# Paged attention: each group's latent page request in two halves, the second behind a key turn

## What is computed

```python
ckv_past = cache_ckv[l, page_table].reshape(db, past_len, KV_LORA)      # 8 x 8192 x 256
kr_past = cache_krope[l, page_table].reshape(db, past_len, MLA_ROPE)    # 8 x 8192 x 32

def mla_sample_attention(q_nope, q_rope, c_kv, k_rope, ckv_past, krope_past, w_uk, w_uv):
    q_lat = jnp.einsum('bthn,lhn->bthl', q_nope, w_uk)
    s_past = (jnp.einsum('bthl,bpl->bhtp', q_lat, ckv_past)
              + jnp.einsum('bthr,bpr->bhtp', q_rope, krope_past))
    ...
    s = jnp.concatenate([s_past, s_new], axis=-1) * scale
    p = jax.nn.softmax(s, axis=-1)
    lat = (jnp.einsum('bhtp,bpl->bthl', p[..., :P], ckv_past)
           + jnp.einsum('bhts,bsl->bthl', p[..., P:], c_kv))
    return jnp.einsum('bthl,lhv->bthv', lat, w_uv)
```

## Time and profile before

| | |
|---|---|
| time before, median of 3 runs | 1907.12 us (1905.14 to 1908.0) |
| the profiled execution's own time | 1910.69 us |
| its span, first to last instruction | 1908.8 us |
| PE busy | 1827.8 us, 96% of the span |
| PEld busy | 1587.6 us, 83% |
| DVE busy | 1216.4 us, 64% |
| POOL busy | 567.0 us, 30% |
| DMA, whole span | 176.72 MB, mean 93 GB/s |
| of it the page requests (software queue) | 75.50 MB, 10.5% of 16 engines' span |
| DMA while pages come | 314 to 324 GB/s in five slices of 47.7 us |

### The profile page before, as it was taken

How to read it: one execution, slowest core, us unless ns; L and a number is a source line. 1 busy time by engine, 2 the same in 40 slices (tenths; PEclk the granted TensorE clock), 3 DMA queues, 4 the chain that set the end, 5 groups by cost and what they waited for, 6 DMA issues and landing times.

```text
span 1908.8 us, 34292 instructions
## 1 busy us (share of the span) xinstructions
PE 1827.8 (96%) x14782; PEld 1587.6 (83%) x14782; DVE 1216.4 (64%) x1563; ACT 569.3 (30%) x978; POOL 567.0 (30%) x392
## 2 busy tenths in 40 slices
PE   7999999898998999989998899999999999999998
PEld 6989889885664444449997699999999999999998
DVE  5587776565877887874332756873675276375475
ACT  5222321353553454452121531120111021011026
POOL 2222122240001343422224533333332333333530
PEclk9999999998999999999999999999999999999999
DMA  7121122141002888853134511112111211211202
GB/s 245 45 57 45 47 57 45 39 123 48 1 1 91 324 320 314 315 188 104 30 89 143 177 56 45 46 39 61 45 41 42 63 39 34 61 45 43 79 23 92
DMA packets 162307, 176.72 MB, mean 93 GB/s; under 512 B 21982, under 2 KB 146932, under 8 KB 157772
## 3 DMA queue, kind: packets, MB, share of 16 engines
q1 hardware_dynamic: 146240, 93.54, 16.7%
q0 software_dynamic: 7168, 75.50, 10.5%
q10 hardware_dynamic: 8750, 5.49, 1.0%
HBM read 161.33 MB, written 13.27 MB: 91 GB/s over the span
## 4 chain that ended last, share of the span: by engine, by line
PE 87%; DVE 7%; issue 3%; ACT 1%; DMA 1%; POOL 1%; SPq 0%; ACTq 0%; DVEq 0%; POOLq 0%
PE PS L799 21%; PE PS L801 20%; PE PS L800 20%; PE PS L1120 4%; PE PS L836 4%; PE PS L1162 3%; PE PS L1014 2%; PE PS L1107 1%; PE PS L1142 1%; PE PS L1055 1%; PE PS L1131 1%; PE PS L881 1%; PE PS L987 1%; PE PS L1335 1%; PE PS L1337 1%
## 5 line engine op out<-in xcount | busy, mean ns | idle before, releaser
L737 POOL CAST whi<-wraw 128x1024 fp32r<-128x1024 f32 (+4 forms) x142 | 137.4, 968 | 915.8 <-PE PS L801 860.0
L799 PE MATMUL PS<-BH,whi 128*128 128x344 f32 x1152 | 368.9, 320 | 0.0
L800 PE MATMUL PS<-BL,whi 128*128 128x344 f32 x1152 | 367.1, 319 | 0.0
L801 PE MATMUL PS<-BH,wlo 128*128 128x344 f32 x1152 | 367.0, 319 | 0.0
L739 POOL TENSOR_TENSOR wlo<-wraw,whi 128x1024 fp32r<-128x1024 f32 (+4 forms) x142 | 311.2, 2192 | 11.4
L800 PEld LDWEIGHTS PS<-BL,whi 128*128 128x128 f32 x1152 | 216.2, 188 | 0.5 <-issue 0.5
L799 PEld LDWEIGHTS PS<-BH,whi 128*128 128x128 f32 x1152 | 216.2, 188 | 0.5 <-issue 0.5
L801 PEld LDWEIGHTS PS<-BH,wlo 128*128 128x128 f32 x1152 | 216.2, 188 | 0.0
L799 PE MATMUL PS<-XH,whi 128*128 128x344 f32 x528 | 179.0, 339 | 3.4 <-DVE XL L1911 3.4
L2391 DVE TENSOR_TENSOR XT<-PS,XT 128x1032 f32<-128x1032 f32 x48 | 59.2, 1233 | 175.9 <-PE PS L801 175.8
L800 PE MATMUL PS<-XL,whi 128*128 128x344 f32 x528 | 170.1, 322 | 0.0
(11 more groups left out here) (451 smaller groups left out, 3713.5 us busy)
## 6 DMA issues: line engine op xcount, KB each, us to landing
wraw<-in_w_up_dram SPq DMA_DIRECT2D x44, 512.0 KB, 3.9
wraw<-in_w_in_dram SPq DMA_DIRECT2D x20, 512.0 KB, 4.0
wraw<-in_w_down_dram SPq DMA_DIRECT2D x24, 256.0 KB, 2.9
wraw<-in_w_down_dram SPq DMA_DIRECT2D x16, 320.0 KB, 3.3
xt_kept<-XT SPq DMA_DIRECT2D x1, 4128.0 KB, 12.8
XT<-xt_kept SPq DMA_DIRECT2D x1, 4128.0 KB, 13.9
xstage<-in_x_prompt_dram SPq DMA_DIRECT2D x8, 512.0 KB, 10.4
wraw<-in_w_out_dram SPq DMA_DIRECT2D x8, 512.0 KB, 4.2
```

The source lines that it names most:

```text
L737: gp.tensor_copy(hi, raw).then_inc(w_hi_done, 1)
L799: pe.matmul(out, wh[:, t, 0:m], hi[:, tile(t), s], start=(t == first), stop=False)
L800: pe.matmul(out, wh[:, t, 0:m], low, start=False, stop=False)
L801: ins = pe.matmul(out, wl[:, t, 0:m], hi[:, tile(t), s], start=False, stop=(t == last))
```

## The change

The latent rows of a group are asked for in two requests in place of one. The view of `cache_ckv` now has rows of 8 tokens (8 KB) in place of 16 (16 KB), so a partition's 16 tokens are two rows next to each other; `idx_part[0]` and `idx_part[1]` hold their numbers. The rotary keys are asked for first, with the old `idx`, then the first half of the tokens, then, after an additional wait, the second half. For groups 5 and up that wait is for `kp_turned` to reach 5 (g - 2) + 1: DVE's first key pair of group g - 2 is turned. `sequence_values`, where it is due, stands between the two halves. `page_in` now counts to 48 a group in place of 32, so DVE waits for all three requests.

```diff
+        PARTS = 2
         idx = keep("idx", [P, GT], I32)
+        idx_part, row_part = [keep(f"idx_part{n}", [P, GT], I32) for n in range(PARTS)], keep("row_part", [P, PARTS])
...
-            ckv_rows = i["cache_ckv"][0].rearrange("n (a t) l -> (n a) (t l)", t=GP)
+            ckv_rows = i["cache_ckv"][0].rearrange("n (a t) l -> (n a) (t l)", t=GP // PARTS)
             kr_rows = i["cache_krope"][0].rearrange("n (a t) r -> (n a) (t r)", t=GP)
...
-                at_ = bass.IndirectOffsetOnAxis(ap=idx[:, g:g + 1].bitcast(U32), axis=0)
-                for dst, rows in ((rc, ckv_rows), (rk, kr_rows)):
-                    gp.indirect_dma_start(out=dst[g % SLOTS][:, :, :].rearrange("p t l -> p (t l)"), out_offset=None, in_=rows,
-                                          in_offset=at_).then_inc(page_in[g % SLOTS], 16)
+                request(g, rk, kr_rows, idx, 0, GP)
+                for part in range(1):
+                    load_part(g, part)
+
+            def load_part(g, part):
+                request(g, rc, ckv_rows, idx_part[part], part * GP // PARTS, (part + 1) * GP // PARTS)
+
+            def request(g, dst, rows, rows_at, t0, t1):
+                at_ = bass.IndirectOffsetOnAxis(ap=rows_at[:, g:g + 1].bitcast(U32), axis=0)
+                gp.indirect_dma_start(out=dst[g % SLOTS][:, t0:t1, :].rearrange("p t l -> p (t l)"), out_offset=None,
+                                      in_=rows, in_offset=at_).then_inc(page_in[g % SLOTS], 16)
...
                             load_pages(g)
                         if g >= SLOTS and (g - SLOTS) % NG == NG - 1:
                             sequence_values(gp, step, (g - SLOTS) // NG)
+                        if g < GT:
+                            if g >= SLOTS:
+                                gp.wait_ge(kp_turned, 5 * (g - 2) + 1)
+                            load_part(g, 1)
...
+            for n in range(PARTS):
+                step(ve.tensor_scalar(row_part[:, n:n + 1], rowof[:, 0:1], float(PARTS), float(n), ALU.mult, ALU.add))
+                ve.tensor_scalar(idx_part[n][:, :], bank("idx")[:, 0:GT], 8.0 * PARTS, row_part[:, n:n + 1], ALU.mult, ALU.add)
             take(ve.tensor_scalar(idx[:, :], bank("idx")[:, 0:GT], 8.0, rowof[:, 0:1], ALU.mult, ALU.add))
...
-                ve.wait_ge(page_in[g % SLOTS], 32 * (g // SLOTS + 1))
+                ve.wait_ge(page_in[g % SLOTS], 48 * (g // SLOTS + 1))
```

## The result

The changed kernel takes 1927.7 us (median of 4 runs, 1923.6 to 1930.8), the kernel before 1907.6 us (1905.1 to 1910.1): a ratio of 1.0101, 95% interval 1.0083 to 1.0119, 20 us slower. It lies in the range, on the side of rival (a), 18 us above the forecast. The profiled executions took 1923.59 us (span 1921.8) and 1910.69 us (span 1908.8), 13 us apart: each lies at the near end of its own runs. The traces explain these 13 us; where the other 7 are, they don't show.

A forecast was written before the change was run, and what follows sets the result against it. PE was taken to set the pace, not pages. Terms 0 + 0 + 0 + 2.1 + 0 = +2.1 us, all from sequence closings, gave 1907.1 + 2.1 = 1909.2 us; range 1896 to 1932 us.

The forecast's parts named there:

- rival (a): The third request costs PE 0.2 to 1.2 us in each of 27 groups, 1917 to 1932 us; chance 0.27.
- The third request's own effect on PE: From group 5 on, PE is slowly fed for 1.25 us, but matmuls in stock cover it: 0.
- The bound of 0 to 0.85 us a group: Third request's price if PE has no matmuls in stock: more likely 0.85 us, at most 1.21; 0 to 23 us over 27 groups.
- two requests cost 1.21 us: L1120's last 44 matmuls take 2.50 us in groups with page requests and 1.29 us without.
- The sign that I gave for being wrong: The forecast is wrong if the 2.5 us of L1120's last 44 matmuls change by more than 0.1 us either way.
- The start: Groups 2 to 4: nine requests for six, 3.75 us more of POOL, PE's slowness reaching L1142 where it waits for ACT: 0.
- Where a sequence closes: In six groups additions stand between the halves; second half 0.30 us behind them, next group's first request 0.35 later: 2.1 us.
- The waits for pages and the row numbers: Pages from group 5 on still land before DVE's turn; four added DVE instructions, about 0.8 us, hide in idle time: 0.
- the cover: Time between a group's last page data landing at 709.9 and DVE's turn at 718.63: 8.6 us.
- Rival (c): Pages become the bound, as each request starts its transfer with a gap: 84 us slower less 9, 1982 us; chance 0.02.
- Rival (b): PE's slowing grows with a request's bytes, so moving half away from L1120 makes it faster: 1894.6 us; chance 0.16.
- SBUF: two separate sides: Skill rule that PE never waits for a DMA or GpSimd: added requests cost PE 0 in place of 2.1 us.

The follow-up runs named there:

- a3: The changed kernel with groups 0 to 4 requested whole in two requests each, as before the change: 1917.4 us, ratio 1.0058.
- a4: The changed kernel with latent rows in one request of 16 KB rows and the keys in two halves of 1 KB rows: 1919.4 us, ratio 1.0063.

## Why the prediction was off

**The third request's own effect on PE: "I take 0".** This step failed: the stretch is 10.0 us longer, of which some 7 us are no closing's. I looked for the price in PE's feed of small matmuls and found stock enough. In two of three kinds of group that held: L1133 stayed at 2.50 us and L1175 at 1.93. What I had not looked at is PE's signal to ACT: the request delays it, ACT copies late, and PE waits 0.6 us at L1175. The bound of 0 to 0.85 us a group held it, and rival (a) gave +10 us at 0.3 us a group; the stretch has 10.0, but that the numbers agree is luck, since it isn't 27 groups by 0.3 us but 7 or 8 by 0.6, the closings and four irregular groups. The price was named as a longer L1131 or L1162; it was neither, but a wait between them. That two requests cost 1.21 us was right as a row, but not as 0.6 each: by L the first is free and each later one costs its own 1.25 us, as long as it starts well ahead of the turns. The sign that I gave for being wrong, L1120's 2.50 us changing by 0.1, stayed silent in most groups: it watched the matmuls and not the signal.

**The start: "I add 0".** It failed by 4.9 us, a quarter of the loss. I saw that PE's slowness would reach L1142 and said that PE waits for ACT there; but ACT was waiting for PE's L1144, 13.1 us instead of 9.1, and PE's idling was followed by the lower clock for 10.3 us (before for 3.4). a3 shows it to be the requests.

**Where a sequence closes: 0.35 us, six times.** The mechanism held, with 0.53 for 0.35 in five of the six and 0.27 in the sixth: 2.9 us instead of 2.1. The second half comes 0.15 us behind the additions, sooner than my 0.30, but the next group's keys start 0.65 us after it and not 0.30.

**The waits for pages and the row numbers: 0.** Both right (the cover is 718.63 - 709.9 = 8.7 us, not 8.6): no page is waited for, and a3 has its start back with the row numbers in it. Rival (c) did not come. Rival (b) fell with a4: bytes don't set the price that the third request has.

**"SBUF: two separate sides"** in the Trainium skill's "SBUF — State Buffer" would have the requests cost PE nothing. On the first chip the rows disagree by 1.2 us a group; on the second and third they disagree by 0.2 (1.48 and 1.49 against 1.29 us).

Not foreseen at all, and not foreseeable from one trace: the loss is a matter of the chip. The same two kernels differ by 1.0% on one and by nothing on another (each chip was measured at one time only). That the measured 1927.7 lies in the range is in part luck too: the traces explain 13 of its 20 us.

## What to carry to other kernels

Count a GpSimd request by its place before its bytes: on the chips where requests are dear, a second or third one that starts while PE runs a row of small matmuls cost its own 1.25 us, one just before PE signals another engine 0.6 us, and one beside the longer matmuls of L1175 nothing; so splitting a request needs a place for the new one, at the start of the pipeline too. When a queued instruction is moved behind a wait, list what stands behind it in that queue and who waits for that: here a kernel with an expected gain of 33 us lost 31, on a chip where some 5 were to be had. And compare two versions on more than one chip before a difference of 1% is believed to be the kernel's.

## What the hardware showed unexpectedly

- PE's turns start 2.8 us after the start of the last request that is well ahead of them on two chips and 1.8 us on two others, with POOL's request at 0.94 us on both. The kernel before takes 1908 or 1885 us accordingly. What makes the difference, and what stops PE at all, no row shows; nor was it tried with requests from another engine's queue.
- A request delays PE's signals as well as its matmuls: the turns' news reached ACT 0.6 us later.
- In groups 14 to 22 PE's stream has gaps of 0.6 us and more with only one request a group, and they end 1.2 to 1.6 us after an instruction packet's end. "Runtime: NRT & Kernel Launch" of the Trainium skill, section "Instruction fetch mechanics", says that PE's instructions come by its own DMA queue in blocks of 16 KiB and that this is mostly hidden. The queue q8 fits the size (118 packets, 1.93 MB in the kernel before). In most groups it is hidden here; in those with gaps the times speak against it, though no experiment tried it.
